# The end of a state space mixer: heads in groups of four, and their operands turned earlier

## The reference

```python
u = rms_norm(h, norm1_g)
P = u @ w_in                               # z | xbc | dt | r k v wd ad gd
xbc = silu(causal_depthwise_conv(xbc))     # xs (2048), Bm and Cm (4 groups x 128)
dt = softplus(dt_raw + dt_bias)            # 32 heads
# chunked state space, equal to: for head hd of group g, in token order
#   y[l] = sum over s <= l of (Cm[l] . Bm[s]) * exp(cs[l] - cs[s]) * dt[s] * x[s]
y = y + D_skip * xh
y = y * silu(z)                            # the gates' layer makes z
y_ssd = grouped_rms_norm(y) * norm_g       # 4 groups of 512
y_rwkv = rwkv7_mixer(...)                  # 32 heads of 64, a recurrence over tokens
h = h + concat([y_ssd, y_rwkv]) @ w_out
h = h + (silu(v @ w_gate) * (v @ w_up)) @ w_down,  v = rms_norm(h)
```

## Time and profile before

| | |
|---|---|
| median of 3 runs | 3189.41 us (3189.28 to 3194.16) |
| profiled execution | 3187.53 us, its span 3185.4 us |
| TensorE busy | 2967.0 us, 93% of the span |
| VectorE, ScalarE, POOL busy | 67%, 49%, 22% |
| mean granted clock of TensorE | 0.975 |
| DMA | 475.20 MB, 149 GB/s on the mean |

### The profile page before, as it was taken

The page is one execution under the profiler, slowest core; times in us unless marked ns, Lnnn a source line. Parts: engine busy times, 40 slices in busy tenths (PEclk is TensorE's granted clock), DMA queues, the critical chain, the costliest instruction groups (busy, mean ns, idle before and its releaser), DMA issues.

```text
span 3185.4 us, 50274 instructions
## 1 busy us (share of the span) xinstructions
PE 2967.0 (93%) x19942; PEld 2651.2 (83%) x19942; DVE 2137.2 (67%) x3465; ACT 1572.4 (49%) x2606; POOL 714.3 (22%) x885
## 2 busy tenths in 40 slices
PE   4876999999999997899999899888999999999998
PEld 4865998888888887788888788766788888888887
DVE  8787877765777557667766666555756665566655
ACT  3445555543555444455555555344544444344443
POOL 5356402210112000765555410000100111001100
PEclk9987999999999999999999999998999999999999
DMA  4411555556555555322222222422555555555554
GB/s 178 161 67 40 168 176 189 194 171 198 200 186 186 167 166 175 119 79 91 87 87 87 94 90 100 166 80 90 174 181 176 187 194 171 190 211 186 189 170 144
DMA packets 78953, 475.20 MB, mean 149 GB/s; under 512 B 8129, under 2 KB 11201, under 8 KB 37441
## 3 DMA queue, kind: packets, MB, share of 16 engines
q1 hardware_dynamic: 76480, 459.66, 42.5%
q10 hardware_dynamic: 2240, 12.32, 1.1%
HBM read 465.66 MB, written 6.29 MB: 148 GB/s over the span
## 4 chain that ended last, share of the span: by engine, by line
PE 75%; DVE 13%; ACT 7%; issue 2%; POOL 2%; DMA 0%; ACTq 0%; DVEq 0%; SPq 0%; POOLq 0%
PE bank L692 33%; PE bank L696 22%; PE bank L694 5%; PE bank L695 4%; DVE m L1185 3%; ACT m L2006 2%; PE bank L708 1%; DVE m L1839 1%; PE bank L994 1%; POOL m L2679 1%; POOL m L2675 1%; PE bank L995 1%; PE bank L1109 1%; PE bank L991 1%; PE bank L997 1%
## 5 line engine op out<-in xcount | busy, mean ns | idle before, releaser
L696 PE MATMUL bank<-m,m 128*128 128x256 f32 x6864 | 1932.0, 281 | 0.0
L692 PE MATMUL bank<-m,m 128*128 128x512 f32 x4736 | 1656.6, 394 | 2.5 <-ACT m L2497 2.0
L1185 DVE TENSOR_TENSOR m<-m,m 128x1024 fp32r<-128x1024 f32 (+1 forms) x944 | 1076.7, 1149 | 615.0 <-ACT m L2006 609.0
L696 PEld LDWEIGHTS bank<-m,m 128*128 128x128 f32 x6864 | 1302.5, 190 | 1.2
L2006 ACT ACTIVATE m<-m 128x1024 fp32r<-128x1024 f32 (+1 forms) x944 | 911.8, 979 | 724.0 <-PE bank L696 697.4
L692 PEld LDWEIGHTS bank<-m,m 128*128 128x128 f32 x4736 | 890.0, 188 | 200.8 <-issue 2.5
L694 PE MATMUL bank<-m,m 128*128 128x256 f32 x2128 | 643.4, 302 | 74.2 <-DVE m L1185 67.2
L695 PE MATMUL bank<-m,m 128*128 128x256 f32 x2128 | 607.7, 286 | 0.0
L694 PEld LDWEIGHTS bank<-m,m 128*128 128x128 f32 x2128 | 413.6, 194 | 104.5 <-issue 87.8
L695 PEld LDWEIGHTS bank<-m,m 128*128 128x128 f32 x2128 | 414.2, 195 | 3.6 <-issue 1.9
L2656 POOL TENSOR_TENSOR m<-m,m 128x256 fp32r<-128x256 f32 x44 | 63.4, 1441 | 695.6 <-ACT m L2228 695.6
(11 more groups left out here) (368 smaller groups left out, 3057.5 us busy)
## 6 DMA issues: line engine op xcount, KB each, us to landing
m<-in_w_up SPq DMA_DIRECT2D x88, 1024.0 KB, 4.8
m<-in_w_down SPq DMA_DIRECT2D x128, 704.0 KB, 4.0
m<-in_w_gu SPq DMA_DIRECT2D x88, 1024.0 KB, 4.9
m<-in_w_out SPq DMA_DIRECT2D x48, 1024.0 KB, 5.0
m<-in_w_krv SPq DMA_DIRECT2D x48, 1024.0 KB, 4.8
m<-in_w_xbc SPq DMA_DIRECT2D x24, 1024.0 KB, 4.9
m<-in_w_z SPq DMA_DIRECT2D x16, 1024.0 KB, 4.8
m<-in_w_in SPq DMA_DIRECT2D x14, 1024.0 KB, 4.9
```

What stands on the lines that cost most here:

```text
L692: pe.matmul(bank.rearrange("p (a b) -> p a b", a=2), hi, x, start=kc == L.k0, stop=False)
L696: m = pe.matmul(ps, lo, x[:, 0, :], start=False, stop=last)
L1185: v.tensor_tensor(lo_of(k), raw_of(k)[0], hi_of(k).bitcast(F32), SUB).then_inc(*lo_v(("lo", k)))
```

## The change

It has four parts.

1. A chain of `turn_dt`, `turn_cb` and 13 of the 16 `turn_x` runs inside `second_mixer`, from round 228 (`CLOSING`), one step a round. `turn_cb` now comes ahead of `turn_x`.
2. The heads run in eight quads of two pairs, one quad started every fourth half tile of `L_z`. A quad has TensorE's four selections at its step 0 and the heads' products at its step 3; VectorE's differences at step 1, products with the scores at step 2 (one instruction of 128x768 a pair), skip and gate at step 4; ScalarE's Exp at step 1 (one of 128x768 a pair). Silu is taken for two gate tiles at a time.
3. The waits for the last stores of `ysave` go from ahead of `L_z` to a step inside it (VectorE at tile 5, ScalarE at step 6, ahead of the load).
4. `L_outr` follows `L_z` in one chain of steps: the halves of y are made in two groups of eight, ahead of its steps 0 and 1, the load of `h` is issued at its step 1, VectorE waits for it when it closes a tile, and the norms start at its steps 4, 7, 10 and 13.

```diff
+CLOSING = PAIRS + 8 * ROUNDS + 12
+def last_mixer(main, quad, turn, norm, *more):
+    quads = [timed(*((8 * j + 4 * p, quad(2 * j + p)) for j in range(4))) for p in range(2)]
+    norms = timed(*((36 + 3 * g, norm(g)) for g in range(4)))
+    run(mix(*((g, 1) for g in more), (main, 1), (quads[0], 1), (quads[1], 1), (timed((3, turn)), 1), (norms, 1)))
...
 # TensorE
-            second_mixer(main(), block, tail, after, iter(range(8)), last_squares(sums_))
-            turn_dt()
-            run(mix((linear(L_z, nrhs, lambda kc: cut_of(N_two, kc), free=following(L_x[1], 7),
-                            done=zdone.add), 1),
-                    (chain(turn_x(), turn_cb(), flight(ssd_pair, 16, 2)), 3)))
-            run(mix((linear(L_outr, ...), 3), (norm_ssd(), 1)))
+            second_mixer(main(), block, tail, after, iter(range(8)), last_squares(sums_),
+                         timed((CLOSING, chain(turn_dt(), turn_cb(), turn_x(0, 13)))))
+            gates = linear(L_z, nrhs, lambda kc: cut_of(N_two, kc), free=following(L_x[1], 7))
+            sums = linear(L_outr, ...)
+            last_mixer(chain(gates, sums), quad, turn_x(13, 16), norm_ssd)
...
+            def quad(q):
+                for i in (2 * q, 2 * q + 1):
+                    b = banks[6 + i % 2]
+                    if q:
+                        pe.wait_ge(*ssd_v["d", i - 2])
+                    for e in range(2):
+                        hd = 2 * i + e
+                        m = pe.matmul(b[:, e * T:e * T + T], ident[96:128, 96 + hd:97 + hd].broadcast_to([32, 128]),
+                                      cs_[96:128, :], start=True, stop=True)
+                    m.then_inc(*ssd_pe(("sel", i)))
+                yield
+                yield
+                yield
+                for i in (2 * q, 2 * q + 1):
+                    yb, w = banks[4 + i % 2], sw[i % 2]
+                    pe.wait_ge(*ssd_v["w", i])
+                    pe.wait_ge(*ssd_v["xd", i])
+                    if q:
+                        pe.wait_ge(*ssd_v["s", i - 2])
...
+                yield
 # VectorE
+            def quad(q):
+                yield
+                for i in (2 * q, 2 * q + 1):
+                    b, w = banks[6 + i % 2], sw[i % 2]
+                    v.wait_ge(*ssd_pe["sel", i])
...
+                yield
+                for i in (2 * q, 2 * q + 1):
+                    w = sw[i % 2]
+                    v.wait_ge(*ssd_a["w", i])
+                    v.wait_ge(*ssd_v["cb", i // 4])
+                    v.tensor_tensor(w, w, cbm[:, i // 4, :].unsqueeze(1).broadcast_to([128, 2, 384]), MUL).then_inc(
+                        *ssd_v(("w", i)))
+                yield
+                yield
...
-            for b in (5, 6, 7):
-                v.wait_ge(st_y[b % 3], 16 * (b // 3 + 1))
-            turn_dt()
             def z_done(t):
+                if t == 5:
+                    for b in (6, 7):
+                        v.wait_ge(st_y[b % 3], 16 * (b // 3 + 1))
+            last_mixer(chain(linear(L_z, z_done), linear(L_outr, sum_done)), quad, turn_x(13, 16), norm_ssd,
+                       timed((32, halves_of_y())))
 # ScalarE
+            def quad(q):
+                yield
+                for i in (2 * q, 2 * q + 1):
+                    a.wait_ge(*ssd_v["d", i])
+                    a.activation(sw[i % 2], sw[i % 2], ACT.Exp).then_inc(*ssd_a(("w", i)))
+                yield
+                yield
+                yield
+                yield
             def z_done(t):
+                if t % 2:
+                    for i in (t - 1, t):
+                        a.wait_ge(*ssd_v["zs", i])
+                        a.activation(z[:, i, :], z[:, i, :], ACT.Silu).then_inc(*ssd_a(("z", i)))
+            last_mixer(chain(linear(L_z, z_done), linear(L_outr, lambda t: None)), quad, iter(range(3)), norm_ssd,
+                       timed((6, load_y()), (32, halves_of_y())), timed((33, load_h())))
```

More of the change, by code:

```diff
@@ L539, in program @@
         xd = alloc(2, 2048)
-        sw = [alloc(384) for _ in range(4)]
+        sw = [alloc(2, 384) for _ in range(2)]
         yl = alloc(16, T)
         sw2 = [alloc(T) for _ in range(2)]
+        cbm = alloc(4, 384)
+        dtT, csT = alloc(2, 32), alloc(2, 32)
         vvr = within(hno, 2, 16, T, dt=F32R)
@@ L1080, in turn_x @@
                     yield
[L1082 to L1089, removed]
-                yield
@@ L1116, in norm_ssd @@
[L1116 to L1119, removed]
+                    for e in range(2):
+                        pe.matmul(yb[HALVES[e], 0:256], xd[:, 0, i * 128 + e * 64:i * 128 + e * 64 + 64],
+                                  w[:, e, 0:256], start=True, stop=False)
+                    for e in range(2):
+                        m = pe.matmul(yb[HALVES[e], 128:256], xd[:, 1, i * 128 + e * 64:i * 128 + e * 64 + 64],
+                                      w[:, e, 256:384], start=False, stop=True)
@@ L1177, in vector_program @@
         def vector_program(v):
-            cuts, zdone, turned = [0], set(), set()
+            cuts, turned = [0], set()
             def cut_to(j):
@@ new lines, in halves_of_y, with norm_ssd @@
+            def halves_of_y():
+                for n in range(2):
+                    for i in range(8 * n, 8 * n + 8, 2):
+                        v.wait_ge(*ssd_a["vv", i])
+                        v.tensor_tensor(vvr[:, 1, i, :], yl[:, i, :], vvr[:, 0, i, :].bitcast(F32), SUB).then_inc(
+                            *ssd_v(("vv", i)))
+                    yield
+            def norm_ssd(g):
+                if g == 0:
+                    v.wait_ge(*ssd_g["vv", 15])
+                    v.wait_ge(*ssd_v.last)
+                norm(N_ssd[g])
+                yield
@@ L1963, in vector_program, with sum_done @@
             v.tensor_scalar(omka, WR("rwkv_k_a_2"), -1.0, 1.0, MUL, ADD).then_inc(*once_v(("omka",)))
-            second_mixer(main(), block, tail, after, steps_dt(), both_rates(ffn_v.last))
-            for b in (5, 6, 7):
-                v.wait_ge(st_y[b % 3], 16 * (b // 3 + 1))
-            turn_dt()
+            second_mixer(main(), block, tail, after, steps_dt(), both_rates(ffn_v.last),
+                         timed((CLOSING, chain(turn_dt(), turn_cb(), turn_x(0, 13)))))
             def z_done(t):
+                if t == 5:
+                    for b in (6, 7):
+                        v.wait_ge(st_y[b % 3], 16 * (b // 3 + 1))
                 v.wait_ge(*lin_pe["tile", L_z.number(t)])
                 v.tensor_tensor(z[:, t, :], banks[t % 2][:, 0:T], rl, MUL).then_inc(*ssd_v(("zs", t)))
[L1972 to L1982, removed]
+            def sum_done(t):
+                v.wait_ge(ld_h, 16)
+                residual("wkv", L_outr)(t)
+            last_mixer(chain(linear(L_z, z_done), linear(L_outr, sum_done)), quad, turn_x(13, 16), norm_ssd,
+                       timed((32, halves_of_y())))
             out = Lag(L_outs, residual("ssd", L_outs), lambda t: None, low(N_ffn2))
@@ L1995, in scalar_program @@
         def scalar_program(a):
-            cuts, zdone = [0], set()
+            cuts = [0]
             def cut_to(j):
@@ new lines, in z_done, with load_y, halves_of_y @@
+            def z_done(t):
+                if t % 2:
+                    for i in (t - 1, t):
+                        a.wait_ge(*ssd_v["zs", i])
+                        a.activation(z[:, i, :], z[:, i, :], ACT.Silu).then_inc(*ssd_a(("z", i)))
+            def load_y():
+                for b in (5, 6, 7):
+                    a.wait_ge(st_y[b % 3], 16 * (b // 3 + 1))
+                a.dma_start(yl, d["ysave"]).then_inc(ld_y, 16)
+                yield
+            def halves_of_y():
+                a.wait_ge(*lin_pe["tile", L_z.number(15)])
+                a.wait_ge(ld_y, 16)
+                for n in range(2):
+                    for i in range(8 * n, 8 * n + 8):
+                        a.activation(vvr[:, 0, i, :], yl[:, i, :], ACT.Copy).then_inc(*ssd_a(("vv", i)))
```

166 lines of the change are left out of this document (60 added, 106 removed).

## The result

The changed kernel takes 3139.64 us (median of four runs, 3138.18 to 3140.09) against 3189.49 us before: ratio 0.984, 95% interval 0.9828 to 0.9853, or 50 us less. The forecast was 3152 with a range of 3128 to 3174. Its direction held, and in the main its mechanism; the gain was 12 us larger than forecast.

A forecast was written before the change was run, and what follows sets the result against it. Waits in the gates' layer L_z, no engine's sum, were taken as the bound. 3187.5 + 7 - 12 - 38 + 5.6 = 3150, with the runs' median 1.9 us higher: 3152 us, range 3128 to 3174.

The forecast's parts named there:

- Part 1: End of RWKV: turned inputs and scores moved there lengthen VectorE's loop per tile; +7 us, bounds 0 and 12.
- Part 2: Start of L_z: TensorE's stand-still, put down to VectorE and ScalarE waiting for ysave stores, goes; -12 us, bound -9.
- Part 3: L_z itself: quads cycle in 17.9 us with a 1.6 us wait, three clock falls; 147 us against 185.1, -38.
- Part 4: Boundary from L_z to L_outr: halves of y come later, second step waits 2.5 us more; +5.6 us, bounds 3 and 9.
- TensorE becomes the bound: Rival, L_z: ScalarE and VectorE keep ahead, no 1.6 us waits, no clock falls; 3131 us, chance 0.15.
- Clock at every quad: Rival, L_z: TensorE's clock falls at every quad, 14 us more; 3166 us, chance 0.17.
- costly turning: Rival, end of RWKV: turning costs 12 us and each of 18 rounds waits 0.5 us more; 3166 us, chance 0.10.
- Slower: Rival, L_z: quads out of step with half tiles, TensorE waits for cut pieces; 25 us cycle gives 3209, chance 0.04.

The follow-up runs named there:

- experiment 3: Changed kernel, but VectorE and ScalarE again wait for all ysave stores ahead of the gates' layer L_z; 3142.3 us (0.9853).
- experiment 2: Changed kernel, but each pair's products with xd go head by head, as in the kernel before; 3138.3 us (0.9842).
- head_wide: Changed kernel with Exp and the product with the scores one head at a time (128x384), steps unchanged; 3139.3 us (0.9843).
- experiment 6: Changed kernel with Exp and the product with the scores one head at a time, the same run as head_wide; 3139.3 us (0.9843).
- experiments 8 and 9: 8: changed kernel, halves of y in one group, 3139.0 us. 9: products_later, sums closed a tile later, 3123.4 us; also halves in one group, 3123.6 us.
- products_later: Changed kernel, but a quad's products, skip and gate come one half tile later, except in the last quad; 3124.6 us (0.9795).
- old_heads: Changed kernel with the earlier kernel's heads: one after another, pairs two at a time in flight, Silu tile by tile; 3210.0 us (1.0066).
- experiment 5: Changed kernel with the heads of the kernel before, the same run as old_heads; 3210.0 us (1.0066).
- experiment 1: Changed kernel, but a quad's products, skip and gate one half tile later except in the last quad, the same run as products_later; 3124.6 us (0.9795).
- sums_later: products_later, but VectorE adds each tile of the output layer's first half to h one tile later; 3123.4 us (0.9793).

## Why the prediction was right, and where its sizes were off

**Part 1 held.** +7 forecast, +5.3 measured. The tiles of RWKV's end take 7.2 to 7.6 us, near the forecast 7.5; VectorE in the changed kernel, one tile from scaling to scaling:

```profile
2016.43 0.42 DVE L1844 TENSOR_TENSOR m<-bank,m 128x256 f32<-128x256 f32 x1
2017.59 1.52 DVE L1848 SCALAR_TENSOR_TENSOR m<-m,m,m 128x255 f32<-128x255 f32 x3 [0.74 <-ACT m L2393]
...
2020.55 1.23 DVE L1194 TENSOR_TENSOR m<-m,m 128x1024 fp32r<-128x1024 f32 x1 [1.43 <-ACT m L2029]
...
2024.01 0.42 DVE L1844 TENSOR_TENSOR m<-bank,m 128x256 f32<-128x256 f32 x1
```

7.6 us, with the same idle times of 0.74 and 1.4 us ahead of taps and cuts as in the earlier trace rows: the turns add to the loop as reckoned.

**Part 2 was drawn too simply.** There is no stand-still left and TensorE begins its first selections at 2040.48. But the 12 us can't be put down to the stores: experiment 3 gives them 3 to 5 us beside quads. The step that failed is that the 11.4 us wait had one cause, the stores. It had two, the stores and a turned input next in TensorE's order, and with the turned input taken away most of it goes though the stores' waits stay.

**Part 3 was right in kind, mis-sized by 15 us.** From the first selections to the end of L_z: 147 us forecast, 132.2 measured. The widths were priced right; VectorE and ScalarE in one quad of the changed kernel:

```profile
2100.00 0.42 DVE L1998 TENSOR_TENSOR m<-bank,m 128x256 f32<-128x256 f32 x1 [2.19 <-PE bank L705]
...
2104.88 1.23 DVE L1194 TENSOR_TENSOR m<-m,m 128x1024 fp32r<-128x1024 f32 x1 [1.86 <-ACT m L2029]
2106.03 1.82 DVE L1920 TENSOR_TENSOR m<-m,m 128x768 f32<-128x768 f32 x2
...
2116.76 0.42 DVE L1998 TENSOR_TENSOR m<-bank,m 128x256 f32<-128x256 f32 x1 [2.20 <-PE bank L705]
```

```profile
2101.76 0.85 ACT L2430 ACTIVATE m<-m 128x768 f32<-128x768 f32 x1 [4.27 <-DVE m L1913]
2103.06 0.85 ACT L2430 ACTIVATE m<-m 128x768 f32<-128x768 f32 x1 [0.45 <-DVE m L1913]
2103.81 1.99 ACT L2029 ACTIVATE m<-m 128x1024 fp32r<-128x1024 f32 x2
```

Two masked products take 1.82 us (0.95 each, overlapping), an Exp 0.85, and the order is the forecast one: gates, differences, Exp, Exp, copies, cut, products. The wait came out at 1.44 us (1.6 forecast). Two terms were off. The quad's products were "2.8" and are 1.67: the two heads of a pair run together (experiment 2), and I had added up single heads. With the shorter wait that makes the cycle 16.76 us instead of 17.9, 8 us over seven cycles. The clock was to fall three times for 8 us; it fell once in L_z, for about 1.7 us (the first two windows under "The clock"), 6 us less.

What the prediction didn't single out is how much of the gain is TensorE's own work. From the end of the 11.4 us wait to the end of L_z TensorE was busy 159.0 of 185.1 us before, from the first selections on 120.2 of 132.2 us after. The idle time fell by 14 us. Of the busy time, 32.3 us lay at the lower clock before and 3.4 after; reckoned as half lost, that is another 14 us (an estimate; a 64-column record takes 1.12 us there and 0.65 at the upper level). The remaining 24 to 25 us are work that TensorE no longer has in this stretch. The heads make most of it: 1.42 us for each of 32 before, 45 us, and 1.67 and 1.99 for each of eight quads after, 29 us (an estimate from these rows). Most of the rest are the turned inputs and scores, now under RWKV, and the last quad's products, now behind L_z. No run separates this saving from that of the fixed steps.

**The clock.** Windows of 3 us of the changed kernel (TensorE busy, granted clock, DMA share, GB/s), around the first quad's wait of 3.20 us, two later waits of 1.44, and the boundary:

```profile
2054.00:2057.00 3.00, 1.99 (x12) 0.66 0.61 164
2057.00:2060.00 3.00, 3.00 (x23) 0.77 0.46 191
2087.00:2090.00 3.00, 1.84 (x16) 1.00 0.00 0
2105.00:2108.00 3.00, 1.56 (x16) 1.00 0.29 44
...
2177.00:2180.00 3.00, 2.26 (x7) 0.64 0.17 68
...
2186.00:2189.00 3.00, 3.00 (x11) 0.50 1.08 462
```

The waits of 1.44 us, every 16.76 us, left the clock at its upper level; the one of 3.20 us did not, nor did 1.91 and 3.09 us close together at the boundary. The rule of the Trainium skill weighed in the prediction, that frequent micro-idles make the clock swing, did not show at this size. Waits of 1.6 us, which I had taken to cost a fall in three of eight cases, didn't either: head_wide has them, and its granted clock is 1.00 from 2060 to 2175 us (experiment 6).

**Part 4 was too cheap.** +5.6 forecast, +10.1 measured. The second step is late as described, waiting 3.09 us where I had 2.5; but I priced the waits alone and not the clock behind them. From 2177 to 2192 TensorE is granted 0.64, 0.79, 0.78, 0.50 and 0.59, which costs about 5 us, where the 0.81 of the earlier trace rows had cost 1.7. The second step ends 18.1 us after L_z, where I had 14.7. By the end of L_outr the difference to the kernel before is 9.1 us; the last 1 us is no more than the profiles of the runs differ from there to their end (849.6 to 850.6 us). In experiments 8 and 9 three such moves at this boundary gained nothing; what stays open is whether an earlier load of h together with earlier halves would.

**The rivals.** "TensorE becomes the bound" was wrong for the change and right for products_later, which removes exactly the 1.44 us waits it rests on: 3124.6, against the 3131 I gave it. "Clock at every quad" and "costly turning" fell. "Slower" fell for the change: TensorE's only wait for a cut piece in L_z is 0.4 us. old_heads is slower, but by waits for masked decays, not by the waits for pieces that this rival names.

**Luck.** The four parts missed by -2, 0, -15 and +4.5 us, so part 4's miss hid some of part 3's, and the -12 of part 2 came out for a cause described only in half.

Where the 50 us come from, then: the quads in L_z, shown by experiment 5, which takes them back; not the width (2.4 us), not the pairing of Silus (0.8), not the stores alone (3 to 5). Within the quads, experiment 1 shows what one step of distance is worth (12 to 15 us); how much is the fixed steps and how much TensorE's smaller work is estimated above and not tested. The turning under RWKV adds 8. Since these don't add up one by one, no finer division is given. The best kernel of this study is products_later, or sums_later at 3123.4: 65 us under the kernel before.

## What to carry to other kernels

With in-order queues, write one cycle out engine by engine before counting busy time: here no engine's sum was the bound in L_z, and four heads' work, grouped and moved to fixed steps, made up most of 50 us, a further half tile of distance 12 to 15 more. Count as well what grouping does to the work itself: heads one by one took 1.42 us each, in quads 0.92 each. Where a consumer waits a little in every cycle, issue it one step later rather than make its producer faster: 1.44 us a quad went away with a `yield`, while width and table loads had given next to nothing. Price a boundary with its clock: behind the two waits there (1.91 and 3.09 us) the lower clock cost about 5 us, and a wait removed there came back at the next instruction that needed the same queue.

## What the runs showed of the hardware

Two heads' fp32 products of 64 columns each, into the two halves of the output partitions, take 0.87 us together (2107.03 to 2107.90) and 0.79 for one alone between selections (2096.70 to 2097.49), in either order of issue (experiment 2). Two that stand side by side but write the same half take 0.70 and 0.74 us one after the other (before, 2103.67). An ACTIVATE starts 0.01 us after the 1.28 us load of its table ends (2098.76 + 1.28, then 2100.05). Waits of TensorE of 1.44 us at a spacing of 16.76 us left its granted clock at 1.00, and so did head_wide's of 1.54 to 1.61 us; one of 3.20 us was followed by 0.66 and 0.77 in the next windows of 3 us.
